# Moving a per-token norm factor from the inputs of the up projections into their sums in PSUM

## What is computed

```python
def rms_norm(x, g):
    xf = x.astype(jnp.float32)
    y = xf * lax.rsqrt(jnp.mean(xf * xf, -1, keepdims=True) + EPS)
    return (y * g.astype(jnp.float32)).astype(x.dtype)

def conv_ffn(x, w_up, conv_w, conv_b, w_down):
    u = x @ w_up                       # 256 x 5632
    ...
    c = conv_b
    for j in range(CONV_W):            # 3 taps along the tokens
        c = c + conv_w[j] * up[:, j:j + s]
    g, val = c[..., :FFN_HIDDEN], c[..., FFN_HIDDEN:]
    return (jax.nn.gelu(g) * val) @ w_down

    h = h + rms_norm(a, norm_g[i, 1])
    f = conv_ffn(rms_norm(h, norm_g[i, 2]), ffn_w_up[i], ...)
    h = h + rms_norm(f, norm_g[i, 3])
```

## Time and profile before

| | us |
|---|---|
| median of 3 runs | 1065.12 |
| lowest and highest | 1064.92, 1067.35 |
| profiled execution, its own time | 1066.56 |
| its span | 1064.8 |
| PE busy | 1036.0 |
| DVE busy | 663.6 |
| ACT busy | 560.7 |
| POOL busy | 417.6 |

### The profile page before, as it was taken

How to read it: one execution, slowest core, us unless ns; L and a number is a source line. 1 busy time by engine, 2 the same in 40 slices (tenths; PEclk the granted TensorE clock), 3 DMA queues, 4 the chain that set the end, 5 groups by cost and what they waited for, 6 DMA issues and landing times.

```text
span 1064.8 us, 21773 instructions
## 1 busy us (share of the span) xinstructions
PE 1036.0 (97%) x8216; PEld 950.1 (89%) x8216; DVE 663.6 (62%) x1074; ACT 560.7 (53%) x1022; POOL 417.6 (39%) x283
## 2 busy tenths in 40 slices
PE   9899999999999999999999999999999999999997
PEld 7799699999978998699999987899999899999996
DVE  4555767677665665776766755766676555554545
ACT  4555665555555555756555565644443355554433
POOL 1000234433351334334333463865653365534431
PEclk9999999999999999999999999999999999999999
DMA  8333465665543443365656434333213245546551
GB/s 317 120 124 128 132 218 186 195 197 178 177 159 130 140 147 131 114 225 183 205 184 201 159 102 148 110 120 109 92 61 120 80 133 149 155 137 209 199 181 43
DMA packets 46136, 162.27 MB, mean 152 GB/s; under 512 B 5248, under 2 KB 5504, under 8 KB 45952
## 3 DMA queue, kind: packets, MB, share of 16 engines
q1 hardware_dynamic: 44784, 156.78, 45.1%
q0 software_dynamic: 1296, 4.72, 1.4%
HBM read 160.43 MB, written 1.05 MB: 152 GB/s over the span
## 4 chain that ended last, share of the span: by engine, by line
PE 90%; DVE 3%; POOL 3%; ACT 2%; issue 1%; DMA 1%; DVEq 0%; SPq 0%; ACTq 0%
PE work L399 14%; PE work L401 14%; PE work L400 14%; PE work L1688 9%; PE acc L399 6%; PE acc L400 6%; PE acc L401 6%; PE work L2410 4%; PE work L2422 2%; PE acc L2422 2%; POOL low L368 1%; PE acc L1939 1%; PE acc L1953 1%; PE acc L1955 1%; POOL stat L559 1%
## 5 line engine op out<-in xcount | busy, mean ns | idle before, releaser
L368 POOL TENSOR_TENSOR low<-raw,high 128x1024 fp32r<-128x1024 f32 x109 | 265.7, 2441 | 293.4 <-ACT high L357 290.9
L368 DVE TENSOR_TENSOR low<-raw,high 128x1024 fp32r<-128x1024 f32 (+2 forms) x184 | 273.2, 1493 | 159.3 <-ACT high L357 159.2
L357 ACT ACTIVATE high<-raw 128x1024 fp32r<-128x1024 f32 (+2 forms) x293 | 299.5, 1032 | 43.9 <-DMA raw<-in_w_out 29.1
L399 PE MATMUL work<-xh,high 128*128 128x256 f32 (+1 forms) x1032 | 290.0, 281 | 0.7 <-DVE low L368 0.7
L400 PE MATMUL work<-xl,high 128*128 128x256 f32 (+1 forms) x1032 | 287.9, 279 | 0.0
L401 PE MATMUL work<-xh,low 128*128 128x256 f32 (+1 forms) x1032 | 287.8, 279 | 0.0
L399 PEld LDWEIGHTS work<-xh,high 128*128 128x128 f32 (+1 forms) x1032 | 193.2, 187 | 7.6 <-issue 4.8
L400 PEld LDWEIGHTS work<-xl,high 128*128 128x128 f32 (+1 forms) x1032 | 193.3, 187 | 2.0 <-issue 0.3
L401 PEld LDWEIGHTS work<-xh,low 128*128 128x128 f32 (+1 forms) x1032 | 193.3, 187 | 0.2
L1156 POOL TENSOR_TENSOR h<-gelu,cv 128x256 f32<-128x256 f32 x44 | 50.5, 1149 | 198.7 <-ACT gelu L1077 102.0
L1688 PE MATMUL work<-xh,high 128*128 128x256 f32 x256 | 76.7, 300 | 0.0
(11 more groups left out here) (385 smaller groups left out, 2201.2 us busy)
## 6 DMA issues: line engine op xcount, KB each, us to landing
raw<-in_w_ffn SPq DMA_DIRECT2D x132, 512.0 KB, 4.3
raw<-in_w_out SPq DMA_DIRECT2D x39, 512.0 KB, 4.5
raw<-in_w_att SPq DMA_DIRECT2D x32, 512.0 KB, 3.7
raw<-in_w_diff SPq DMA_DIRECT2D x31, 512.0 KB, 4.3
raw<-in_w_gdn SPq DMA_DIRECT2D x24, 512.0 KB, 4.0
raw<-in_w_mla SPq DMA_DIRECT2D x8, 512.0 KB, 3.6
raw<-in_w_gdnz SPq DMA_DIRECT2D x8, 512.0 KB, 3.6
raw<-in_w_mla SPq DMA_DIRECT2D x8, 384.0 KB, 3.1
```

The lines of the kernel that those rows point to most:

```text
L357: act.activation(high[k][:, 0:w], raw[k][:, 0:w], ACT.Copy).then_inc(high_done[k], 1)
L368: eng.tensor_tensor(low[k][:, 0:w], raw[k][:, 0:w], high[k][:, 0:w], ALU.subtract).then_inc(low_done[k], 1)
L399: pe.matmul(out, lhs[0], rhs[0], start=start, stop=False)
```

## The change

The two feed-forward inputs are no longer multiplied by the factor per token. `hid` itself is transposed, as soon as each half of it is there; ScalarE copies the high part with the channel's gain as its scale, and VectorE makes the low part with the same gain. Each block is now 128 channels by 256 tokens. The factor is computed beside this: two columns of it are broadcast to 128x128 (`factor_cols_dve`), TensorE turns them into a 128x256 tile with two matmuls in the middle of the second up projection (`factor_pe`), and VectorE copies that to `hn` (`factor_dve`).

In every step VectorE multiplies each of the four up sums by the factor, in place in PSUM, before ScalarE's middle tap and its own outer taps. The tap semaphores count three for each sum instead of two. The low splits of the two left-over chunks move from ahead of the first step to behind the first gate sum's multiply. The pre-norms ahead of the diff mixer and the last layer stay as they were; of the four gain loads two go away, and a padding and a small vector table grow.

```diff
-    def project_t(pe, out, k, width=P, offset=0, x=None, blocks=KB, arriving=None):
+    def project_t(pe, out, k, width=P, offset=0, x=None, blocks=KB, arriving=None, between=None):
         for b in range(blocks):
-            if arriving is not None and b % 4 == 0:
+            if arriving is not None and arriving % 2 and b % 2 == 0:
+                pe.wait_ge(n_["xl"], 4 * arriving + 1 + b // 2)
+            elif arriving is not None and b % 4 == 0:
                 pe.wait_ge(n_["xl"], 4 * arriving + 2 + b // 2)
+            if between is not None and b == blocks // 2:
+                between()
...
+    def raw_pe(pe, n):
+        pe.wait_ge(g["const"], 48)
+        spin(pe, W[3][:], 4)
+        for t in range(NT):
+            for half in range(2):
+                if (t, half) == (0, 1):
+                    spin(pe, W[3][:], 3)
+                pe.wait_ge(n_["hid"], 4 * (n - 1) + 2 * t + half + 1)
+                for b in range(4):
+                    at = (4 * half + b) * P
+                    last = pe.transpose(raw_turned(4 * half + b)[:, t * P:(t + 1) * P], hid[:, t, at:at + P], ident)
+                last.then_inc(n_["turned"], 1)
+                if (t, half) == (1, 0):
+                    spin(pe, acc[:, 3, :], 1)
+        spin(pe, acc[:, 3, :], 1)
...
+    def raw_split_act(act, n, half):
+        act.wait_ge(n_["turned"], 4 * n + 2 + half + 1)
+        for b in range(4 * half, 4 * half + 4):
+            ins = act.activation(xh[:, b, :], raw_turned(b), ACT.Copy, scale=raw_gain(n, b))
+            if b % 2:
+                ins.then_inc(n_["xh"], 1)
+
+    def raw_split_dve(dve, n):
+        for b in range(KB):
+            if b % 2 == 0:
+                dve.wait_ge(n_["xh"], 4 * n + b // 2 + 1)
+            ins = dve.scalar_tensor_tensor(xl[:, b, :], raw_turned(b), raw_gain(n, b), xh[:, b, :], ALU.mult,
+                                           ALU.subtract)
+            if b % 2:
+                ins.then_inc(n_["xl"], 1)
...
+    def factor_cols_dve(dve, n):
+        for t in range(NT):
+            dve.wait_ge(n_["root"], 2 * n + t + 1)
+            dve.tensor_scalar(factor_col[t], cst("ones"), stat[:, 8 + t:9 + t], None, ALU.mult).then_inc(n_["hn"], 1)
+
+    def factor_pe(pe, n):
+        pe.wait_ge(n_["hn"], 4 * (n - 1) + 2)
+        for t in range(NT):
+            last = pe.matmul(acc[:, 3, t * P:(t + 1) * P], factor_col[t], ident, start=True, stop=True)
+        last.then_inc(n_["hn"], 1)
+
+    def factor_dve(dve, n):
+        dve.wait_ge(n_["hn"], 4 * (n - 1) + 3)
+        dve.tensor_copy(factor, acc[:, 3, 0:TOK]).then_inc(n_["hn"], 1)
+        dve.wait_ge(n_["hn"], 4 * (n - 1) + 4)
...
+    def boundary_raw_act(act, n, p, k):
+        post_act(act, n, p, k)
+        pre_square(act, n + 1, 0)
+        raw_split_act(act, n + 1, 0)
+        pre_square(act, n + 1, 1)
+        raw_split_act(act, n + 1, 1)
+
+    def boundary_raw_dve(dve, n, p, k):
+        post_dve(dve, n, p, k)
+        raw_split_dve(dve, n + 1)
+        pre_mean(dve, n + 1, 1)
+        factor_cols_dve(dve, n + 1)
...
     def boundary_pool(pool, n):
...
-        if n < 3:
+        if n == 1:
             pool.wait_ge(n_["hn"], 4 * n + 4)
-            pool.dma_start(pre_gain[:], dram["pre_gain"][n + 1]).then_inc(n_["gain"], 16)
+            pool.dma_start(pre_gain[:], dram["pre_gain"][1]).then_inc(n_["gain"], 16)
...
     def ffn_act(act, layer):
...
-                act.wait_ge(used[bank], p.base[bank] + i + 1)
+                act.wait_ge((s["g_tap"], s["v_tap"])[value], 3 * (i + done) + 1)
...
-            act.wait_ge(f[j]["g_tap"], 2 * (i + done) + 2)
+            act.wait_ge(f[j]["g_tap"], 3 * (i + done) + 3)
             act.activation(gelu[j][:], cg[j][:], ACT.Gelu_apprx_tanh).then_inc(f[j]["gelu"], 1)
...
     def ffn_dve(dve, layer, left_over):
...
+                dve.wait_ge(used[bank], p.base[bank] + i + 1)
+                if isinstance(i, int) and i == 0 and j == 0 and not value:
+                    factor_dve(dve, 2 * layer + 1)
+                dve.tensor_tensor(W[bank][:, 0:TOK], W[bank][:, 0:TOK], factor, ALU.mult).then_inc(tap, 1)
+                if isinstance(i, int) and i == 0 and j == 0 and not value:
+                    left_over()
                 dve.wait_ge(mid, i + done + 1)
                 dve.scalar_tensor_tensor(c[:, 1:TOK], W[bank][:, 0:TOK - 1], ffn_taps(layer, i, j, value, 0, 0),
                                          c[:, 1:TOK], ALU.mult, ALU.add).then_inc(tap, 1)
...
+        def after_first_gate():
+            refill(lo_of(dve), ph["mla"], 2, HEADS - 1)
+            split_low(dve, False, ph["ffn0"], 4, 0)
+        ffn_dve(dve, 0, after_first_gate)
```

More of the change, by code:

```diff
@@ L207, in lay_out @@
     out["post_gain"] = np.ascontiguousarray(np.broadcast_to(post[:, None], (5, P, D)))
[L208 removed]
+    out["pre_gain"] = np.ascontiguousarray(np.broadcast_to(pre[2::2, None], (2, P, D)))
     def chunks(name, parts):
@@ L544, in pre_norm @@
         if t == 0 and half == 0:
-            dve.wait_ge(n_["gain"], 16 * n)
+            dve.wait_ge(n_["gain"], 16 * (n // 2))
         c = cols(half)
@@ new lines, in raw_turned, with raw_gain @@
+    def raw_turned(b):
+        return work[:, b // 2, (b % 2) * TOK:(b % 2) * TOK + TOK]
+    def raw_gain(n, b):
+        return vcol("ffn_gain", (n // 2) * KB + b, 1)
+    def raw_split_act(act, n, half):
[12 more added lines that the diff above has]
+                ins.then_inc(n_["xl"], 1)
@@ new lines, in build @@
+    factor_col = [hn[:, t, 0:P] for t in range(NT)]
+    factor = hn[:, 0, 512:512 + TOK]
+    def factor_cols_dve(dve, n):
[7 more added lines that the diff above has]
+        last.then_inc(n_["hn"], 1)
@@ L1029, in up @@
                 if not (isinstance(i, int) and i + done == 0):
-                    pe.wait_ge(f[j]["g_tap"] if gate else f[j]["v_tap"], 2 * (i + done))
-                first = isinstance(i, int) and i == 0 and j == 0 and gate
-                project_t(pe, W[bank][:, 0:TOK], bank, arriving=2 * layer + 1 if first else None).then_inc(used[bank], 1)
+                    pe.wait_ge(f[j]["g_tap"] if gate else f[j]["v_tap"], 3 * (i + done))
+                n, first = 2 * layer + 1, isinstance(i, int) and i == 0 and j == 0
+                project_t(pe, W[bank][:, 0:TOK], bank, arriving=n if first and gate else None,
+                          between=(lambda: factor_pe(pe, n)) if first and not gate else None).then_inc(used[bank], 1)
         def down(j, i, start=False, stop=False):
@@ L1105, in ffn_act, with ffn_dve @@
         refill(split, p, 5, FFN_STEPS - 1)
-    def ffn_dve(dve, layer):
+    def ffn_dve(dve, layer, left_over):
         p = (ph["ffn0"], ph["ffn1"])[layer]
@@ L1119, in block @@
                                          c[:, 1:TOK], ALU.mult, ALU.add).then_inc(tap, 1)
-                dve.wait_ge(tap, 2 * (i + done) + 1)
+                dve.wait_ge(tap, 3 * (i + done) + 2)
                 dve.scalar_tensor_tensor(c[:, 0:TOK - 1], W[bank][:, 1:TOK], ffn_taps(layer, i, j, value, 2, 0),
@@ L1152, in hidden @@
             pool.wait_ge(s["gelu"], i + done + 1)
-            pool.wait_ge(s["v_tap"], 2 * (i + done) + 2)
+            pool.wait_ge(s["v_tap"], 3 * (i + done) + 3)
             if not (isinstance(i, int) and i + done == 0):
@@ L2957, in _, with after_first_gate @@
         diff_dve(dve)
[L2958 to L2961, removed]
+        boundary_raw_dve(dve, 2, ph["diff_last"], 2)
+        def after_first_gate():
+            refill(lo_of(dve), ph["diff_last"], 2, 0)
+            split_low(dve, False, ph["ffn1"], 4, 0)
+        ffn_dve(dve, 1, after_first_gate)
         post_dve(dve, 3, ph["ffn1"], 5)
```

20 lines of the change are left out of this document (9 added, 11 removed).

## The result

The changed kernel takes 1173.77 us (median; 1173.56 to 1173.94), the kernel before 1065.69 beside it: a ratio of 1.1012, 95% interval 1.0993 to 1.1031, or +108 us. The forecast was 1156 with a range of 1130 to 1182: slower, in the range, and 17 us short in size (+108 against +91).

A forecast was written before the change was run, and what follows sets the result against it. TensorE's 16.70 us step was the bound, with a VectorE, GpSimd and ScalarE ring at 16.33 beside it. Layers of +45.9 and +44.9, together +90.8 on 1066.56, gave 1157.4, 1155.9 against the median, stated as 1156; range 1130 to 1182.

The forecast's parts named there:

- first half of step 0: Start of each feed-forward layer, behind the boundary: first hl done at 141.7 instead of 139.49, +2.2 us a layer.
- second half of step 0: Outside the loop, before its nine steps: two values' multiplies and handovers add 2 x 1.07 us.
- nine steps: The feed-forward loop: nine steps at 21.05 us, 189.45 in all, +41.4 in the first layer and +40.4 in the second.
- end of the layer: From step 10's hl to VectorE getting the sum: 6.1 us instead of 8.14, -2.0 a layer.
- The ring of VectorE, GpSimd and ScalarE: Handovers in one feed-forward step: 16.33 us beside TensorE's 16.70, growing by 4 x 1.18 to 21.05 us.
- to ScalarE 0.04: Handover from VectorE's multiply to ScalarE's pass: 0.04 us of the 1.18 us per value in the loop.
- The bound of 1.35: Upper end of the added time per value (1.05 to 1.35 us); over some 80 values, -10 to +14 us.
- The matmuls that nobody reads: TensorE's spare matmuls around the boundary's transposes (4, 3 and 1), said to lie in the waits for hid.
- The boundary ahead of the second layer: Start of the second feed-forward layer: same list of instructions as the first, so +2.2 us again.
- A: Rival for the loop: multiplies fit VectorE's waiting, TensorE stays the bound; 1060 to 1069.5 us, chance 0.06.
- B: Rival for the loop: collisions of VectorE's split and GpSimd's h dissolve, 2.97 us a step, 1097 us; chance 0.04.
- C: Rival for the loop: TensorE's clock stays at half for most of a step, up to 1403 us; chance 0.05.

The follow-up runs named there:

- run 1: Kernel before plus one VectorE multiply of the same size into an unused tile for every up sum, nobody waiting for it: 1086.25 us.
- run 3: Changed kernel with the multiply on 16 of the 256 columns only, order and waits kept: 1153.35 us.
- run 5: Changed kernel with three of the four multiplies of a step issued one place earlier on VectorE, ahead of the low split: 1096.36 us.
- run 4: Changed kernel with the feed-forward steps of ScalarE, VectorE and GpSimd written out instead of looped: 1152.14 us.
- run 6: Changed kernel without TensorE's 3 + 1 spare matmuls between the raw transposes at the boundary: 1170.1 us.
- run 7: Changed kernel with GpSimd waiting for the second layer's two factor columns before its split: 1172.61 us.
- run 8: Changed kernel with three spare matmuls ahead of TensorE's wait for hl in the loop: 1174.59 us.
- run 10: run 9 without spare matmuls between the transposes, and with the second mean, factor columns, factor transposes and ScalarE's squares moved: 1072.19 us.
- run 9: run 5 with GpSimd also making the low parts of chunk 4: 1076.79 us.

## Why the prediction came out as it did

Forecast and measured terms, between the ends of hl and the starts of VectorE's first instruction of the post norms before and behind the layer, against the earlier trace rows and the same places of the second layer:

```
                                 layer 1              layer 2
first half of step 0          +2.2  -> +4.95       +2.2  -> +6.65
second half of step 0         +2.1  -> +1.07       +2.1  -> +1.08
nine steps                    +41.4 -> +46.83      +40.4 -> +45.82
first half of step 10         +2.1  -> +2.29       +2.1  -> +1.52
end of the layer              -2.0  -> -1.93       -2.0  -> +0.12
sum                           +45.9 -> +53.2       +44.9 -> +55.2
```

With -1.1 in the rest of the span these make the 107.3 us.

**The mechanism was right.** The ring of VectorE, GpSimd and ScalarE had 0.37 us of room, the multiply puts ScalarE's pass in line, four times in a step, and TensorE comes to wait for hl. Runs 1, 3 and 5 show the three parts of it: work alone +0.96 a step, the width of the multiply one for one, and the order the rest, of which run 5 gets back 4.09 of 4.95 us with all the work kept. The two waits of TensorE that the forecast had in each step (0.7 and 3.6 us) show only once in the layer, at the start of the loop (0.73 before 174.00, 3.74 before 186.31). From then on TensorE comes to the first of the two late from its slow stretch, and one wait is left; in the step shown it is 3.11.

**The step that was mis-sized most:** "to ScalarE 0.04 (from GpSimd it is 0.03 ...)". In the loop it is 0.18, and 0.25 once in a step. A value costs 5.33 / 4 = 1.33 on average, not 1.18: 0.60 a step, 5.4 a layer, 10.8 of the 16.5 us that were missing. I had taken the figure from one pair of engines. Run 4 shows 0.04 once the steps are written out. The bound of 1.35 held it, but with some luck: it allowed 0.15 for this handover, and the room came from the multiply, bounded at 0.48 and measured at 0.42.

**The second:** "The matmuls that nobody reads ... lie in the waits for hid", costed at nothing. They held the transposes back: +2.4 us in the first layer (run 6, which ends its first hl at 142.01, where the forecast had 141.7) and 1.3 in the second. For the same reason the first bank was not full 2.4 us earlier: VectorE's low parts ended at 130.54 and not at 127.95, in run 6 at 128.16. I had 7 spare matmuls in mind as 7 instructions; they are 14.

**The third:** "The boundary ahead of the second layer has the same list of instructions; I take +2.2 again". The instructions are the same, and what lies beside them is not: there GpSimd splits, and the column takes 3.00 us, not 0.3; run 7 gets 1.5 us back, about the 1.7 by which this half is later than the first layer's. The Trainium skill (SBUF — State Buffer, section Who interferes with whom) says that a tensor_scalar can run in a mode that holds the port pair which VectorE and GpSimd share, and that one of the two then stands still for the whole instruction of the other. The two rows agree as to the end: the column ends 0.09 us after GpSimd's split. They leave open why the column was held although its record starts first.

**Smaller ones.** In the second half of step 0 I counted two multiplies; the gate's was long done in the wait for the pass, so it is one (+1.07). The gain at the end of a layer came in the first (8.14 to 6.2 us) and not in the second. There GpSimd makes two splits, 735.70 to 740.42, ahead of its last h, and TensorE waits 3.80 us for hh. The kernel before has the same two splits (627.38 to 632.14) and no such wait, since TensorE still had two down projections to do; that the splits now set the end is read from the order of the trace, and no run tried it.

**The rivals.** A fell with run 1. B did not occur: the split of chunk 4 took 3.28 us and h 1.48. Run 5 shows that another order shortens h and lengthens the split beside it. C: the drop came once and not twice in a step, for 3.5 us in one and 6 in the next, and run 8 shows it free. The rule of the Trainium skill that spoke for C (TensorE: Matmul & The Clock Gate, HAM oscillation) agrees with the trace after the waits of 3.08 to 3.13 us in the first layer, 0.50 to 0.54 over the next 3.5 us, and not after those of 0.57 and 0.73 us, where the clock stayed at 1.00. The time that a cold start takes was covered here.

## What to carry to other kernels

An engine's share of busy time says nothing of its room. Follow the ring of handovers through one step and compare its length with the bound's: here 38% idle meant 0.37 us. An operation put between two engines costs its handovers and the work that now can't run beside it; issue it one place earlier, over work that the next engine can run under, and most of that comes back (21.65 to 17.56 us a step for the same work, a part of it because h then started ahead of a split). And where the same instructions stand at a second place, look at what the neighbour engines do there.

## What the hardware showed unexpectedly

- A handover from VectorE to ScalarE took 0.18 to 0.25 us in the loop and 0.04 where the steps were written out, one from GpSimd to ScalarE 0.03 in the same loop; writing them out took 21.6 us off the changed kernel (run 4).
- A tensor_scalar of 128x128 took 0.29 us alone, 3.00 beside one split of GpSimd, 4.66 and 5.29 beside two (runs 7, 10 and 9), though in two of the three its record starts 0.53 us ahead of the first split's.
- Between h on GpSimd and VectorE's split the one that started first kept its length: h 1.48 and the split 1.21 with the split ahead by 0.31 us, h 0.74 and the split 1.66 with h ahead by 0.16 (run 5).
- TensorE at half clock for 3.5 to 6 us of a step of 21.65 cost nothing (run 8).
